# Hybrid streaming encoder: orders within a step, and the low parts of y's second chunk on GpSimd

## The chip, the cores and the metric

One core of a Trainium2 chip (trn2) runs one program: four layers of an encoder over 2048 positions. The metric is the device time of one execution in microseconds. TensorE (PE) multiplies, VectorE (DVE), ScalarE (ACT) and GpSimd (POOL) do elementwise work, SyncE (SP) issues the DMAs.

## The reference

x is 2048 x 1024, c a vector of 1024; everything is float32. What matters here:

```python
cond = silu(c)
for layer in range(4):          # RG-LRU, gated DeltaNet, causal pooling, windowed attention
    mod = cond @ ada_w[layer] + ada_b[layer]
    shift, scale, gate = split(mod, 3)
    h = rms_norm(x, norm_w[layer]) * (1.0 + scale) + shift
    y = mixer[layer](h)         # input projection, mixer, then y @ w_out (1024 x 1024)
    x = x + gate * y
return rms_norm(x, final_norm_w)
```

## The kernel before

The 2048 positions are done in two halves of 1024; a half lives in SBUF with features on the partitions (x, y and h are 8 tiles of 128 features x 1024 positions), and its positions are cut in two chunks of 512. A half runs through phases, one function each: `residual_phase` with layer -1 takes x in (transposes it and makes the first h), then for each layer a mixer phase (`rg_phase`, `dn_project_phase` and `dn_recur_phase`, `pool_phase`, `swa_phase`) and again `residual_phase`, which does the mixer's output projection, adds it to x, and makes the next layer's h (or, after the last layer, the output). In each phase every engine has its own program in a fixed order, and the engines wait for one another by semaphores; there is no planner. A phase's engines also wait at a fence until the others have left the phase before.

A float32 product of 128 x 128 weights and 128 x 512 activations is made of three matmuls (line 231): each operand is split in a high part (rounded to fp32r by ScalarE) and a low part (the difference), and hi*hi, hi*lo and lo*hi are summed. A projection's output tile ("a product") takes 8 x 3 matmuls. Weights come as tiles of 128 x 1024 through two raw buffers: SyncE loads (`load_to`), ScalarE rounds (`round_to`, line 204, which waits until the product that used the slot three tiles ago is done), GpSimd subtracts (`subtract_to`, line 213). The next raw load waits for that subtraction.

In an output projection (`residual_phase`) the steps j = 0 to 15 are (chunk c, feature tile d). The operand is y, whose high parts `round_y` makes on ScalarE (line 118) and whose low parts `lower_y` makes (line 127): those of the first chunk before the first step, the even tiles on VectorE and the odd on GpSimd; those of the second chunk in steps 0 to 7, one per step, alternating in the same way. Product 8 waits, tile by tile, for these. Products 0 and 1 are made together (line 250). Three PSUM banks are used in turn, so product j waits until product j - 3 has been added to x. In step j VectorE makes its low part if it has one, waits for product j, adds gate * product to x (line 781), adds the square of tile j - 1 to the running total (line 751; ScalarE makes the square, line 868), and in the second chunk makes a tile of the next h (lines 712 and 724). After product 8, TensorE sums the total of chunk 1 over the features (`sum_squares`, line 650, or line 646 after the last layer), for which it waits until square 7 is added.

After the last layer, ScalarE weights each x tile in place (line 870), TensorE turns it back with four transposes (`turn_x`, line 664), and the turn of tile j - 1 stands behind product j from j = 1 on. VectorE and ScalarE take the turned rows in turn, there is one buffer for a square, and the rows are scaled and stored.

The modulation cond @ ada_w is made in the first half by the class `Modulation`: `load` brings pieces of 128 rows of ada_w, `accumulate` has VectorE multiply each by its cond column and add it to a sum (lines 294 and 297), `reduce` has TensorE sum over the partitions (line 305), `finish` adds it to the vectors. It runs beside other work: shift and scale of layer 0 in the first ingest (16 pieces of 128 x 1024, in the space that h takes later), the rest in `rg_phase`, in layer 0's projection (`late`, 48 pieces of 128 x 512, four in each of steps 3 to 14) and in `pool_phase` (64 pieces of 128 x 512).

In `pool_phase` the products go by group g (4), part (u or gate), chunk c and tile t (2). VectorE does for each group the window sums and p of both chunks, each followed by a slot of six modulation pieces, then for each chunk the gate (line 2485), y, and another slot of six. TensorE reuses a gate's bank after line 2485, and makes the group product of p (line 2394) in between. SyncE loads three weight tiles ahead of the fence, the fourth behind it.

## Time and profile before

| | us |
|---|---|
| median of 3 timed runs | 3575.91 (3573.37 to 3576.22) |
| profiled execution | 3569.85 |
| its span | 3568.1 |
| TensorE busy, matmuls | 3316.8 (93%) |
| VectorE busy | 2307.7 (65%) |
| ScalarE busy | 1514.9 (42%) |
| GpSimd busy | 952.0 (27%) |
| mean granted TensorE clock | 0.967 of full |

The profile records one execution. Busy time is the sum of an engine's instructions; an instruction that stands because its engine cannot go on counts as busy too. "PEclk" is the TensorE clock that was granted, as a share of 2.4 GHz (0.5 is 1.2 GHz). In a timeline each instruction has its start and duration, and behind it in brackets the idle time of its engine before it and what released it. PEld is the weight load of a matmul.

### The profile page before, as it was taken

The page shows a single profiled execution, that of the slowest core. Times are in us where ns is not written, and L with a number is a line of the kernel's source. Part 1 is how long each engine was busy: PE and PEld are TensorE (multiplying, and loading weights), DVE is VectorE, ACT ScalarE, POOL GpSimd, SP SyncE. Part 2 cuts the span into 40 slices and gives each one's busy share as a digit, 9 for nine tenths or more (in the row PEclk, how much of TensorE's full clock was granted, in tenths as well). Part 3 has the DMA queues.
Part 4 walks back from the last instruction along what each step waited for, and adds up shares of the span by engine and source line. Part 5 has one row for each costly group of instructions (what it writes and reads, how often), then busy time and mean ns, then how long its engine had stood idle before and what let it go on. Part 6 is the DMA issues. An engine that isn't in the chain of part 4 may idle for free.

```text
span 3568.1 us, 49267 instructions
## 1 busy us (share of the span) xinstructions
PE 3316.8 (93%) x18911; PEld 2680.0 (75%) x18911; DVE 2307.7 (65%) x3812; ACT 1514.9 (42%) x2635; POOL 952.0 (27%) x495
## 2 busy tenths in 40 slices
PE   5998999799999999999889999988999999999998
PEld 3776688677887777888767777876778777788876
DVE  6887888763467765565457767896536564565553
ACT  4665365333344124323466655653334431342234
POOL 1003233211143124222510042432121421422243
PEclk7999899899999999999989999998999999999999
DMA  4434455444743523111231123554449211221112
GB/s 170 132 111 136 120 145 148 124 108 130 263 172 94 162 89 89 49 31 37 71 124 55 46 78 87 153 137 112 126 111 351 81 54 53 65 72 37 36 48 95
DMA packets 569015, 383.83 MB, mean 108 GB/s; under 512 B 67802, under 2 KB 522445, under 8 KB 568781
## 3 DMA queue, kind: packets, MB, share of 16 engines
q1 hardware_dynamic: 568781, 380.68, 35.7%
q8 instruction: 150, 2.46, 0.3%
q14 instruction: 84, 0.69, 0.1%
HBM read 299.01 MB, written 80.54 MB: 106 GB/s over the span
## 4 chain that ended last, share of the span: by engine, by line
PE 70%; DVE 16%; issue 4%; ACT 4%; DMA 4%; SPq 1%; POOL 1%; ACTq 0%; DVEq 0%; POOLq 0%
PE bank L231 52%; DVE dnp_conv L1866 3%; PE bank L250 2%; DVE dnp_diag_term L1944 2%; DVE h_lo L724 1%; PE bank L2394 1%; DVE dnp_diag_inv L1947 1%; PE bank L2603 1%; DMA dn_planes<-dnp_inv_t 1%; PE bank L2644 1%; PE bank L2630 1%; DVE res_h L712 1%; PE bank L1556 1%; DVE res_ada_sums L297 1%; POOL w_lo L213 1%
## 5 line engine op out<-in xcount | busy, mean ns | idle before, releaser
L231 PE MATMUL bank<-h_hi,w_hi 128*128 128x512 f32 x3488 | 1424.6, 408 | 39.3 <-DVE x_res L781 8.9
L231 PE MATMUL bank<-h_hi,w_lo 128*128 128x512 f32 x3488 | 1374.1, 394 | 0.0
L231 PE MATMUL bank<-h_lo,w_hi 128*128 128x512 f32 x3488 | 1373.4, 394 | 0.0
L213 POOL TENSOR_TENSOR w_lo<-w_raw,w_hi 128x1024 fp32r<-128x1024 f32 x262 | 651.4, 2487 | 1438.2 <-ACT w_hi L204 1437.6
L231 PEld LDWEIGHTS bank<-h_hi,w_hi 128*128 128x128 f32 x3488 | 664.5, 191 | 206.6 <-issue 27.9
L231 PEld LDWEIGHTS bank<-h_lo,w_hi 128*128 128x128 f32 x3488 | 665.5, 191 | 142.6 <-issue 12.8
L231 PEld LDWEIGHTS bank<-h_hi,w_lo 128*128 128x128 f32 x3488 | 663.3, 190 | 144.9
L204 ACT ACTIVATE w_hi<-w_raw 128x1024 fp32r<-128x1024 f32 x292 | 307.9, 1054 | 267.1 <-PE bank L231 128.8
L1866 DVE SCALAR_TENSOR_TENSOR dnp_conv<-dnp_raw,dn_conv_w,dnp_conv 128x512 f32<-128x512 f32 x288 | 265.6, 922 | 237.8 <-ACT dnp_conv L1688 230.4
L127 POOL TENSOR_TENSOR h_lo<-y,h_hi 128x512 fp32r<-128x512 f32 x72 | 102.2, 1432 | 501.9 <-ACT h_hi L118 501.3
L127 DVE TENSOR_TENSOR h_lo<-y,h_hi 128x512 fp32r<-128x512 f32 x56 | 100.5, 1814 | 153.8 <-ACT h_hi L118 153.7
L712 DVE SCALAR_TENSOR_TENSOR res_h<-x_res,mod_scale,res_rstd 128x512 f32<-128x512 f32 x128 | 148.2, 1164 | 58.2 <-ACT res_rstd L827 58.2
L781 DVE SCALAR_TENSOR_TENSOR x_res<-bank,mod_gate,x_res 128x512 f32<-128x512 f32 x128 | 94.9, 746 | 131.0 <-PE bank L231 130.7
L868 ACT ACTIVATE res_sq<-x_res 128x512 f32<-128x512 f32 x160 | 100.3, 627 | 142.6 <-DVE x_res L781 97.8
L734 ACT ACTIVATE h_hi<-res_h,mod_shift 128x512 fp32r<-128x512 f32 x128 | 91.9, 724 | 152.7 <-DVE res_h L712 151.7
L2587 POOL TENSOR_TENSOR swa_probs<-swa_probs,swa_tiny 128x1024 f32<-128x1024 f32 x32 | 60.8, 1900 | 335.3 <-DVE swa_tiny L2815 335.3
L1704 ACT ACTIVATE y<-dnp_conv 128x512 f32<-128x512 f32 x96 | 60.8, 633 | 174.0 <-DVE dnp_conv L1866 173.7
L1680 ACT ACTIVATE dnp_raw<-bank 128x512 f32<-128x512 f32 x96 | 56.8, 592 | 176.5 <-PE bank L231 172.9
L751 DVE TENSOR_TENSOR res_sq_total<-res_sq_total,res_sq 128x512 f32<-128x512 f32 x140 | 122.5, 875 | 10.0 <-ACT res_sq L868 9.4
L2788 DVE TENSOR_TENSOR swa_probs<-bank,swa_rel_bias 128x128 f32<-128x128 f32 x128 | 31.0, 285 | 148.7 <-PE bank L2618 148.6
L724 DVE SCALAR_TENSOR_TENSOR h_lo<-res_h,mod_shift,h_hi 128x512 fp32r<-128x512 f32 x128 | 121.6, 950 | 3.7 <-ACT h_hi L734 1.5
L2719 ACT ACTIVATE swa_probs<-swa_probs 128x1024 f32<-128x1024 f32 x32 | 34.0, 1062 | 169.4 <-DVE swa_probs L2805 169.4
(327 smaller groups left out, 4684.2 us busy)
## 6 DMA issues: line engine op xcount, KB each, us to landing
dnr_in<-dn_planes SPq DMA_DIRECT2D x112, 512.0 KB, 7.1
dn_planes<-y SPq DMA_DIRECT2D x192, 256.0 KB, 2.5
w_raw<-in_dn_w_in SPq DMA_DIRECT2D x64, 512.0 KB, 4.5
w_raw<-in_swa_w_in SPq DMA_DIRECT2D x36, 512.0 KB, 3.7
w_raw<-in_rg_w_in SPq DMA_DIRECT2D x32, 512.0 KB, 4.9
w_raw<-in_rg_w_out SPq DMA_DIRECT2D x32, 512.0 KB, 3.8
w_raw<-in_dn_w_out SPq DMA_DIRECT2D x32, 512.0 KB, 3.9
w_raw<-in_pool_w_in SPq DMA_DIRECT2D x32, 512.0 KB, 4.1
```

What stands on the lines that cost most here:

```text
L127: alu.tensor_tensor(self.h_lo[:, k, cols], self.y[:, k, cols], self.h_hi[:, k, cols].bitcast(F32), ALU.subtract).then_inc(self.y_split[k % ...
L204: self.nc.scalar.activation(self.hi[j % SLOTS][:, :, :], self.raw[j % 2][:, :, :], ACT.Copy).then_inc(self.rounded, 1)
L213: alu.tensor_tensor(self.lo[j % SLOTS][:, :, :], self.raw[j % 2][:, :, :], self.hi[j % SLOTS][:, :, :].bitcast(F32), ALU.subtract).then_in ...
L231: ins = self.nc.tensor.matmul(out, w[slot][:, k, :], x[:, k, cols], start=(k == 0 and n == 0), stop=(k == KT - 1 and n == 2))
L250: ins = self.nc.tensor.matmul(out, w[slot][:, k, :], x[:, k, cols], start=(k == 0 and m == 0), stop=(k == KT - 1 and m == 2))
L712: nc.vector.scalar_tensor_tensor(hf[m % NHF][:, :], x[:, k, cs[c]], core.modA[:, col:col + 1], rstd[:, :], op0=ALU.mult, op1=ALU.mult).the ...
L724: nc.vector.scalar_tensor_tensor(h_lo[:, k, cs[c]], hf[m % NHF][:, :], core.modB[:, col:col + 1], h_hi[:, k, cs[c]].bitcast(F32), op0=ALU. ...
L734: nc.scalar.activation(h_hi[:, k, cs[c]], hf[m % NHF][:, :], ACT.Identity, bias=core.modB[:, col:col + 1]).then_inc(s_hi, 1)
L751: nc.vector.tensor_tensor(total[c][:, :], total[c][:, :], sq[j % len(sq)][:, :], ALU.add).then_inc(s_add, 1)
L781: nc.vector.scalar_tensor_tensor(here, ring[j % len(ring)][:, :], core.modG[:, col:col + 1], here, op0=ALU.mult, op1=ALU.add).then_inc(s_x, 1)
L868: nc.scalar.activation(sq[j % len(sq)][:, :], x[:, d, cs[c]], ACT.Square).then_inc(s_sq, 1)
L1866: ins = V.scalar_tensor_tensor(conv[to][:, :], raw[r][:, k:k + CH], tap(par, k, n), conv[to][:, :], op0=ALU.mult, op1=ALU.add)
```

## The change

- In `residual_phase`, VectorE adds square j - 1 ahead of the addition of product j (but square 0 behind product 1), and no longer makes low parts of the second chunk: GpSimd makes all eight, one per step, behind the step's weight tile.
- After the last layer, the turns of tiles 0 and 1 both stand behind product 2; from there the turn of tile j - 1 stands behind product j, as before.
- In the first ingest, the scale of layer 0 is no longer summed on VectorE: its eight pieces of 128 x 1024 are multiplied by TensorE with the cond column as weights (two matmuls of 512 columns a piece, into banks 2 and 6, one piece in each of steps 4 to 11, behind the step's transposes), ScalarE copies the row of 1024, eight matmuls of one column turn it (bank 3), VectorE adds it. Scale and shift pieces are loaded in turn. The reduction of the shift and the turning stand ahead of the last sum of squares on TensorE.
- In `pool_phase`, SyncE loads four weight tiles ahead of the fence, and the modulation's pieces (now seven a slot) begin two slots later, after the first group's first y, with loads and reductions moved along.

```diff
+SCALE_BANKS, SCALE_FROM = (2, 6), 4
@@ residual_phase, sync
-                ada.load(sp, 0, ada.pieces)
+                for k in range(KT):
+                    sp.dma_start(scale_w[k], A["ada_w"][0, k * P:k * P + P, SCALE * D:SCALE * D + D]).then_inc(s_sw[k], 16)
+                    ada.load(sp, k, k + 1)
@@ residual_phase, tensor
+            def multiply_scale(k):
+                pe.wait_ge(s_sw[k], 16)
+                for i, b in enumerate(SCALE_BANKS):
+                    ins = nc.tensor.matmul(core.bank[b][0:1, :], core.cond[:, k:k + 1], scale_w[k][:, i * CH:i * CH + CH],
+                                           start=(k == 0), stop=(k == KT - 1))
+                if k == KT - 1:
+                    ins.then_inc(s_sm, 1)
+
+            def turn_scale():
+                pe.wait_ge(s_sr, len(SCALE_BANKS))
+                for m in range(KT):
+                    ins = nc.tensor.matmul(core.bank[3][:, KT + m:KT + m + 1], scale_row[0:1, m * P:m * P + P],
+                                           core.ones[0:1, 0:1], start=True, stop=True)
+                ins.then_inc(s_sc, 1)
...
+                    if ada and SCALE_FROM <= j < SCALE_FROM + KT:
+                        multiply_scale(j - SCALE_FROM)
...
-                if final and j > TURN_LAG - 1:
+                if final and j == 2:
+                    turn_x(0)
+                if final and j >= 2:
                     turn_x(j - TURN_LAG)
...
+            if ada:
+                for t in range(len(ada.blocks)):
+                    ada.reduce(pe, t)
+                turn_scale()
             if final or ada:
                 sum_squares(NCH - 1)
...
-            if ada:
-                for t in range(len(ada.blocks)):
-                    ada.reduce(pe, t)
@@ residual_phase, vector
-                if not ingest and c + 1 < NCH and d % 2 == 0:
-                    core.lower_y(dve, nc.vector, c + 1, [d])
+                if j > 1 or ingest and j:
+                    add_square(j - 1)
                 if not ingest:
                     dve.wait_ge(*projected(j))
                     here, col = x[:, d, cs[c]], layer * KT + d
                     nc.vector.scalar_tensor_tensor(here, ring[j % len(ring)][:, :], core.modG[:, col:col + 1],
                                                    here, op0=ALU.mult, op1=ALU.add).then_inc(s_x, 1)
-                if j:
-                    add_square(j - 1)
+                if not ingest and j == 1:
+                    add_square(0)
...
-                ada.accumulate(dve, KT, ada.pieces)
+                dve.wait_ge(s_sc, 1)
+                nc.vector.tensor_tensor(core.modS[:, here], core.bank[3][:, KT:2 * KT], core.modS[:, here], ALU.add)\
+                nc.vector.tensor_tensor(core.modA[:, here], core.modS[:, here], core.modA[:, here], ALU.mult).then_inc(s_sd, 1)
@@ residual_phase, scalar
+                act.wait_ge(s_sm, 1)
+                for i, b in enumerate(SCALE_BANKS):
+                    nc.scalar.activation(scale_row[0:1, i * CH:i * CH + CH], core.bank[b][0:1, :], ACT.Copy).then_inc(s_sr, 1)
@@ residual_phase, gpsimd
-                if not ingest and c + 1 < NCH and d % 2:
+                if not ingest and c + 1 < NCH:
                     core.lower_y(pool, nc.gpsimd, c + 1, [d])
@@ pool_phase
-            per = -(-ada.pieces // (4 * (NG - 1)))
+            per = -(-ada.pieces // (4 * (NG - 1) - GT))
...
-            w.load_to(sp, tile0 + 3)
+            w.load_to(sp, tile0 + 4)
...
-                    if ada:
-                        ada.load(sp, max(0, per * i - 3), per * i + 3)
+                    if ada and i >= GT:
+                        ada.load(sp, max(0, per * (i - GT - 1) + 3), per * (i - GT) + 3)
...
-                    if i == 2 * ((KT * m + KT - 1) // per) + 5:
+                    if i == 2 * ((KT * m + KT - 1) // per + GT) + 5:
...
-                    if ada and g < NG - 1:
-                        ada.accumulate(dve, per * (4 * g + c), per * (4 * g + c + 1))
+                    if ada and 0 < g < NG - 1:
+                        ada.accumulate(dve, per * (4 * g + c - GT), per * (4 * g + c - GT + 1))
...
-                        ada.accumulate(dve, per * (4 * g + 2 + c), per * (4 * g + 3 + c))
+                        ada.accumulate(dve, per * (4 * g + c), per * (4 * g + 1 + c))
```

## Rows read from the trace of the kernel before

**Rows 1.** the line of the low parts of y, by engine: duration ns min/median/max
```profile
L127 POOL TENSOR_TENSOR h_lo<-y,h_hi x72: 1268/1294/2344, 276.6 to 3507.9; 128x512 fp32r<-128x512 f32 x72
L127 DVE TENSOR_TENSOR h_lo<-y,h_hi x56: 679/1781/2524, 279.3 to 3499.0; 128x512 fp32r<-128x512 f32 x56
```

**Rows 2.** windows, two projections: start:end us, busy us of PE PEld DVE ACT POOL, PEclk, DMA
```profile
1340.00:1431.00 91.00, 88.96 (x388) 72.38 (x387) 53.90 (x52) 37.15 (x51) 42.64 (x20) 1.00 0.30 87
1712.00:1826.00 114.00, 101.93 (x496) 82.86 (x494) 42.24 (x54) 50.37 (x73) 48.11 (x24) 0.96 0.37 121
```

**Rows 3.** chain of waits, last layer, first half: start us, us, what
```profile
1729.81 7.54 PE bank L231 x24
...
1744.82 5.52 PE bank L231 x24
...
1779.93 6.40 PE bank L231 x24
```

**Rows 4.** timeline of TensorE there: start us, us, instruction [idle before it <- releaser]
```profile
1728.69 0.69 PE L664 MATMUL bank<-ident,x_res 128*128 128x128 f32 x2 [5.44 <-ACT x_res L870]
...
1757.16 0.66 PE L664 MATMUL bank<-ident,x_res 128*128 128x128 f32 x4 [0.91 <-ACT x_res L870]
...
1777.71 0.49 PE L646 MATMUL bank<-ones,res_sq_total 128*128 128x1 f32 x3 [1.44 <-DVE res_sq_total L751]
...
1824.68 0.55 PE L664 MATMUL bank<-ident,x_res 128*128 128x128 f32 x3 [2.34 <-ACT x_res L870]
```

**Rows 5.** timeline of the second half's layer 0: PE, DVE, POOL
```profile
2088.38 0.50 PE L231 MATMUL bank<-h_hi,w_hi 128*128 128x512 f32 x1 [4.04 <-DVE x_res L781]
...
2124.85 0.70 PE L650 MATMUL bank<-res_sq_total,ones 128*128 128x512 f32 x1 [1.44 <-DVE res_sq_total L751]
...
2097.62 2.72 DVE L751 TENSOR_TENSOR res_sq_total<-res_sq_total,res_sq 128x512 f32<-128x512 f32 x1
...
2084.77 2.34 POOL L213 TENSOR_TENSOR w_lo<-w_raw,w_hi 128x1024 fp32r<-128x1024 f32 x1 [8.23 <-ACT w_hi L204]
...
2099.75 1.74 POOL L127 TENSOR_TENSOR h_lo<-y,h_hi 128x512 fp32r<-128x512 f32 x1
...
2121.10 1.29 POOL L127 TENSOR_TENSOR h_lo<-y,h_hi 128x512 fp32r<-128x512 f32 x1
```

**Rows 6.** timeline of the first half's layer 0: PE, DVE, POOL
```profile
351.81 0.80 PE L231 MATMUL bank<-h_hi,w_hi 128*128 128x512 f32 x1 [6.57 <-POOL h_lo L127]
...
412.52 0.80 PE L305 MATMUL bank<-ones,res_ada_sums 128*128 128x1 f32 x3 [6.26 <-DVE res_ada_sums L297]
...
326.83 2.48 DVE L127 TENSOR_TENSOR h_lo<-y,h_hi 128x512 fp32r<-128x512 f32 x1 [0.32 <-ACT h_hi L118]
...
340.89 2.50 DVE L127 TENSOR_TENSOR h_lo<-y,h_hi 128x512 fp32r<-128x512 f32 x1 [0.30 <-ACT h_hi L118]
...
391.20 2.23 DVE L751 TENSOR_TENSOR res_sq_total<-res_sq_total,res_sq 128x512 f32<-128x512 f32 x1
...
390.40 2.49 POOL L213 TENSOR_TENSOR w_lo<-w_raw,w_hi 128x1024 fp32r<-128x1024 f32 x1 [4.61 <-ACT w_hi L204]
```

**Rows 7.** timeline of the first half's pooling layer: PE, DVE
```profile
1148.77 0.50 PE L231 MATMUL bank<-h_hi,w_hi 128*128 128x512 f32 x1 [3.63 <-POOL w_lo L213]
...
1162.58 0.79 PE L231 MATMUL bank<-h_hi,w_hi 128*128 128x512 f32 x1 [4.64 <-DVE pool_silu L2485]
...
1272.36 0.50 PE L231 MATMUL bank<-h_hi,w_hi 128*128 128x512 f32 x1 [0.73 <-DVE pool_silu L2485]
...
1169.64 0.75 DVE L297 SCALAR_TENSOR_TENSOR pool_ada_sums<-pool_ada,vectors,pool_ada_sums 128x512 f32<-128x512 f32 x1 [1.10 <-DMA pool_ada<-in_ada_w]
```

**Rows 8.** timeline of the start of the program: DVE, PE
```profile
49.66 9.62 DVE L297 SCALAR_TENSOR_TENSOR res_ada_sums<-before_h,vectors,res_ada_sums 128x1024 f32<-128x1024 f32 x7
...
63.55 0.75 DVE L712 SCALAR_TENSOR_TENSOR res_h<-x_res,mod_scale,res_rstd 128x512 f32<-128x512 f32 x1
...
45.67 2.08 PE L650 MATMUL bank<-res_sq_total,ones 128*128 128x512 f32 x2 [9.57 <-DVE res_sq_total L751]
```

More of the change, by code:

```diff
@@ L799, in _ @@
             if ada:
[L800 removed]
+                dve.wait_ge(s_sc, 1)
+                here = slice(0, KT)
+                nc.vector.tensor_tensor(core.modS[:, here], core.bank[3][:, KT:2 * KT], core.modS[:, here], ALU.add)\
+                    .then_inc(s_sd, 1)
+                dve.wait_ge(s_sd, 1)
+                nc.vector.tensor_tensor(core.modA[:, here], core.modS[:, here], core.modA[:, here], ALU.mult).then_inc(s_sd, 1)
+                dve.wait_ge(s_sd, 2)
                 ada.finish(dve)
```

11 lines of the change are left out of this document (9 added, 2 removed).

## The prediction

> **What bounds the kernel now.** I read the page first, then the waits of TensorE phase by phase, then the chain of waits and the timelines around each wait. The windows show the pattern: in the output projection of layer 2, TensorE is busy 88.96 of 91 us at full clock, so that only its few waits can be saved; in that of the last layer it is busy 101.93 of 114 at 0.96 [rows 2]. A product (24 matmuls) takes 5.5 us [rows 3]. So the question is which TensorE waits go, what they cost with the clock that they lower, and which new ones come. Every projection has products 0 to 7 (first chunk) and 8 to 15 (second); there are eight, four layers in two halves.
>
> **Last layer, order of TensorE and VectorE (twice).** TensorE now stands 5.44 us before the first turn of x, because product 0 has to be added, squared, weighted first [rows 4]. Product 2 needs none of that (its bank is free) and moves ahead of both turns; by its end ScalarE has done both squares. The wait goes: 5.44. The product behind it took 7.54 instead of 5.52 at the lowered clock [rows 3]: 2.02 more. Before each odd product's turn TensorE waits 0.91 [rows 4], three times per half: VectorE first makes a low part (held up by GpSimd's weight tile) and only then adds product j. With that low part on GpSimd the addition is immediate: 2.73. The sum of squares of chunk 1 waits 1.44 [rows 4], since VectorE adds product 8 before it adds square 7; in the new order square 7 was added while product 8 ran: 1.44, and 0.88 of clock behind it (6.40 against 5.52 [rows 3]). At the end, square 15 no longer waits for the addition of square 14, of the 2.34 [rows 4] some 0.65 (one such addition). What is late next is GpSimd: low part 7 follows weight tile 10 (product 7's end + 1.1 for ScalarE + 2.4 + 1.3 = 4.8), wanted at 5.3 here, as the turn gives half a us. Sum 13.2 per half, 26.4 in all. Bounds: 4.8 per half if the first turns only move their wait, 14.5 if nothing new is late.
>
> **The middle projections.** Layers 1 and 2 in both halves and layer 0 in the second: each has the same 1.44 [rows 5] at the sum of squares. But now the addition of square 7 comes early enough to meet GpSimd between its weight tile and low part 7. What happens then is in the trace: VectorE's addition stood 2.72 us while GpSimd worked, and the GpSimd low part behind it took 1.74 instead of 1.29 [rows 5], 0.45 later. Low part 7 already ends at 2122.39 [rows 5], when product 8 wants it. So 1.44 - 0.45 = 1.0 each, 5.0 together (bounds 3 and 7.2). Apart from that GpSimd's step is 2.4 + 1.3 = 3.7 of 5.5, and hides.
>
> **Layer 0, the fourth product.** It waits 4.04 for x [rows 5], as VectorE starts with a low part. Without it x is there 3.9 earlier, but weight tile 3 is only split at 2084.77 + 2.34 = 2087.11 [rows 5], so 1.2 is won, in the second half (0 to 3 with the clock).
>
> **Layer 0 of the first half.** Here VectorE also sums the modulation, four pieces per step, and is the bound: its low parts of steps 4 and 6 start 14.06 apart [rows 6], where two products and a reduction take 12. In such a pair it is occupied all the time, partly by standing: a weight tile on GpSimd from 390.40 to 392.89, and VectorE's addition from 391.20 to 393.43, that is, until just after it [rows 6]. So the two work in turn. The own time of a low part is 0.68 on VectorE and 1.29 on GpSimd [rows 1], so a pair of steps goes from (0.68 + 1.29) to 2.58 of shared time: +0.6, and up to +2.3 when the addition of x, which ran beside the weight tile, now comes behind the blocked square; 2.5 pairs, +1.5 to +5.6. In the second chunk the same lost overlap is 0 to 0.7 in six steps, 0 to +4.2. Against it: the stream starts 1.7 earlier, and the first sum of squares comes one addition (0.7) earlier. Net -0.9 to +7.4; I take +3.5, the middle, since VectorE never idles there. TensorE's 6.57 wait for low part 7 and the 6.26 at the end [rows 6] stay, as they are VectorE's lateness.
> The Trainium skill ("SBUF — State Buffer", section "SBUF: two separate sides") says that VectorE with two SBUF inputs and a GpSimd operation that reads SBUF exclude each other for the whole instruction. By that rule this layer gets slower; if they shared, it would get faster by some 3.5. It speaks against this part of the change, and the trace agrees with it.
>
> **Pooling layer, first half.** Three waits: 3.63 for weight tile 3, 4.64 and 0.73 for VectorE's gate [rows 7]. The tile is now loaded before the fence and is split when its slot comes free; gone. The second wait comes from twelve modulation pieces ahead of the first gates; they move behind, gone too, with some 2.0 of clock (as in the last layer). That is 11.0. But 64 pieces now lie in ten slots of 7 instead of eleven of 6. A piece costs 0.75, and every fourth waits for its DMA, 1.10 [rows 7]: about 1.1 a piece in the slot, three slots in series ahead of a gate, 3.3. The third group has no slack (0.73 was waited): 4.0. The second has some; I take 1.0 (0 to 3.3), and 0.9 for the clock. Net 11.0 - 5.9 = 5.1 (bounds 2 and 9). The second half has no pieces; counted at nothing.
>
> **Start of the program.** VectorE's scale pieces go: one of 0.74 and seven in 9.62, then reduction and last steps until 63.55, 4.3 after them [rows 8]. Instead TensorE multiplies, 16 matmuls of 512 columns. The trace has such a one as a pair in 2.08 at the low clock and about half at full [rows 8]. TensorE has turned x just before and runs at full clock, so I count 1.7 per step, less than two pieces of weight take to land (2.6); they pace it, to about 41. The first sum of squares stands in the queue behind the fifth of them, 7 us later than now; ScalarE and VectorE resume there and need 1.8 per step. The last shift sum ends near 51.9 (now 48.9), then 4.3 and a second set of eight small matmuls, 3.6: 59.8 against 63.55. The sum of squares of the second chunk, now behind these, has until well after the first low part. I take 3.5 saved; bounds: 6 saved, and 7 lost if all 16 ran at the low clock (33 us).
>
> **Sum.** -26.4 - 5.0 - 1.2 + 3.5 - 5.1 - 3.5 = -37.7. The profiled execution took 3569.85 (span 3568.1 and 1.75 around it): 3532.1. The median of the timed runs is 6.06 above it, so 3538.
>
> **Rivals.**
> The last layer only moves its wait: ScalarE does weight tile and rounding before each square, and the two turns behind product 2 wait for it. Against: its work for steps 0 and 1 adds to 5.5 from the end of product 1, just one product. Then 4.8 per half: 3538 + 16.8 = 3555. Chance 0.12.
> Start and pooling give nothing (low clock in the start, seven-piece slots): 3538 + 8.6 = 3547. Chance 0.13.
> GpSimd and VectorE hardly meet: layer 0 wins 3.5 instead of losing it, pooling wins 9: 3538 - 7.0 - 3.9 = 3527. For it: GpSimd is idle more than half of the time. Chance 0.14.
> Slower: low part 7 becomes the gate of product 8 in all eight projections as it is in the first half's layer 0, 6.57 each [rows 6], 52.6 together: 3591, with the clock more. It decides from the point where GpSimd's step (3.7 and what it stands for VectorE) passes a product's 5.5; it has 1.7 to spare. Chance 0.04.
> The change doesn't reach what binds (the waits named had another releaser behind them): within 7 of before. Chance 0.03.
>
> **Numbers.** The forecast, 3530 to 3545, has 0.54. Runs spread over 2.85 us, so 0.2% (7 us) is what can be told from no change. Faster 0.94, same 0.02, slower 0.04. Range 3525 to 3557: it leaves out the slow case and the far ends.
>
> **What would show it.** In the last layer the 5.44 and the 0.91 are gone and the third product takes 5.5; at each sum of squares no 1.44, but up to 0.6 in front of the last matmuls of product 8. Layer 0 of the first half is 0 to 7 longer. In pooling no wait at the first gates, one of some 4 in the third group. The first projection starts near 62. It is wrong if low part 7 is waited for by more than 1 us in the middle layers, or if product 2 of the last layer waits.

## The result and the profile after

The changed kernel takes 3516.0 us (median of 4, 3511.91 to 3519.31), the kernel before beside it 3574.89: ratio 0.9835, 95% interval 0.9818 to 0.9852. The profiled execution took 3519.31. It is faster, as forecast, but below the range: 3525 was its low end, 3538 the forecast. From profile to profile, where the prediction made its sum, the span goes from 3568.1 to 3517.5 us, -50.6; the medians differ by 58.9; forecast was -37.7.

The two windows of [rows 2], in the changed kernel, from each layer's first matmul (columns as there):

```profile
1329.90:1419.40 89.50, 88.46 (x386) 72.31 (x387) 57.19 (x48) 36.26 (x50) 50.11 (x24) 1.00 0.30 89
1698.60:1802.90 104.30, 101.50 (x518) 83.77 (x516) 58.52 (x54) 53.60 (x78) 58.48 (x28) 0.99 0.42 137
```

These windows and those of [rows 2] do not cover quite the same stretch. From the last layer's first matmul to its last sums, the first half in the kernel before and in the changed one:

```profile
1709.70:1825.17 115.47, 103.40 (x500) 83.95 (x497) 43.25 (x55) 51.25 (x74) 47.76 (x23) 0.96 0.36 117
```

```profile
1698.57:1798.87 100.30, 98.36 (x500) 81.09 (x497) 55.67 (x51) 50.27 (x74) 56.12 (x27) 1.00 0.41 129
```

The same 500 records of matmuls take 5.0 us less at the higher granted clock, and 10.1 us of idle time are gone. The chain of waits there, against [rows 3]:

```profile
1712.11 5.44 PE bank L231 x24
1717.56 0.87 PE bank L674 x8
1718.43 5.46 PE bank L231 x24
1723.89 0.44 PE bank L674 x4
...
1747.69 1.07 ACT w_hi L204
1748.76 0.07 issue
1748.83 2.40 POOL w_lo L213
1751.23 1.70 POOL h_lo L127
...
1753.94 0.79 PE bank L656 x8
1754.73 0.50 PE bank L674 x4
1755.22 5.48 PE bank L231 x24
```

The third product takes 5.44, both turns behind it come without a wait, and product 3 takes 5.46 where a product behind the wait took 7.54. Up to the layer's last turn the one place where other engines hold the chain is low part 7 behind weight tile 10 on GpSimd, as the prediction named it; TensorE's pause there is 0.14 us, too short to be told as a wait in the timeline. The last wait of the layer, 2.34 in [rows 4], is 1.68:

```profile
1798.38 0.66 PE L674 MATMUL bank<-ident,x_res 128*128 128x128 f32 x4 [1.68 <-ACT x_res L906]
```

The timeline of TensorE in both layers 0, against [rows 5] (second half, last two lines) and [rows 6] (first half):

```profile
304.18 0.47 PE L231 MATMUL bank<-h_hi,w_hi 128*128 128x512 f32 x1 [3.69 <-POOL w_lo L213]
...
346.26 0.80 PE L231 MATMUL bank<-h_hi,w_hi 128*128 128x512 f32 x1 [4.63 <-POOL h_lo L127]
349.12 1.22 PE L660 MATMUL bank<-res_sq_total,ones 128*128 128x512 f32 x1 [1.21 <-DVE res_sq_total L781]
...
405.35 1.87 PE L305 MATMUL bank<-ones,res_ada_sums 128*128 128x1 f32 x8 [4.62 <-DVE res_ada_sums L297]
...
2059.82 0.50 PE L231 MATMUL bank<-h_hi,w_hi 128*128 128x512 f32 x1 [2.91 <-POOL w_lo L213]
...
2094.28 0.50 PE L231 MATMUL bank<-h_hi,w_hi 128*128 128x512 f32 x1 [0.61 <-POOL h_lo L127]
```

In the second half the 4.04 has become 2.91 and changed its releaser from x to the weight tile, and the 1.44 at the sum of squares has become 0.61 at the low part, both as forecast; the other middle projections show the same 0.6. In the first half the 6.57 and the 6.26 are 4.63 and 4.62 here, but 6.35 and 9.05, and 5.51 and 4.61, in two more profiles of the changed kernel, so these two waits show no direction. The layer's length does: from its first matmul to its second sum of squares it is 127.8 to 130.2 us in four profiles with the new order and 131.2 to 134.3 in six with the old one. VectorE got earlier there, not later.

In the pooling layer the two waits at the start [rows 7] are gone, and two are there that were not, in all profiles of the changed kernel:

```profile
1201.09 0.50 PE L231 MATMUL bank<-h_hi,w_hi 128*128 128x512 f32 x1 [2.05 <-DVE pool_silu L2524]
...
1260.69 0.80 PE L231 MATMUL bank<-h_hi,w_hi 128*128 128x512 f32 x1 [5.27 <-DVE pool_silu L2524]
```

At the start of the program, against [rows 8], the scale products run at full clock (1.00 from 33 to 42 us). The two matmuls of a piece, which the profile records as four, take 1.88, and there is one piece per 2.4 with the transposes between:

```profile
36.08 0.66 PE L700 MATMUL bank<-ident,y 128*128 128x128 f32 x4
36.67 1.88 PE L681 MATMUL bank<-before_h,vectors 128*1 128x512 f32 x4
...
54.51 3.56 PE L689 MATMUL bank<-ones,res_scale_row 1*128 1x1 f32 x16
...
58.71 1.41 DVE L742 SCALAR_TENSOR_TENSOR res_h<-x_res,mod_scale,res_rstd 128x512 f32<-128x512 f32 x2
```

The norm's first operation starts at 58.71; it was 63.55.

Where the time went, by stretches of TensorE between marks that all kernels have (a projection's first matmul, its sums of squares; lengths read from the starts of these instructions). The third column is the difference of the two first profiles. Since stretches without any edit turned out to move by several us from one profile to the next, the last column takes the mean of two profiles of the kernel before and three of the changed one (the second and third are runs of the experiments below).

| stretch | forecast | first pair | means |
|---|---|---|---|
| start, to the first product | -3.5 | -4.8 | -4.4 |
| layer 0, first half | +3.5 | -2.9 | -2.8 |
| five middle projections (with the fourth product) | -6.2 | -7.8 | -8.4 |
| pooling, first half | -5.1 | -2.7 | -1.7 |
| pooling, second half | 0 | -1.0 | -1.0 |
| last layer, twice | -26.4 | -30.3 | -31.2 |
| stages without an edit, and the rest | 0 | -1.1 | -7.1 |
| sum | -37.7 | -50.6 | -56.6 |

Two and three profiles are few. Each stretch can also be read from every profile, of the experiments below too, in which all or none of its edits are present (5 to 8 profiles without, 4 to 11 with them). That gives -4.7 for the start, -3.3 for layer 0, -8.9 for the middle projections, -0.6 for pooling in the first half and -1.1 in the second, and -28.7 for the last layer.

### The profile page after: what moved, and what is told of

Same layout as the page of the kernel before. It is cut to its first block, busy times and chain, and to the rows that moved or that the text cites. A ratio compares the mean times of both kernels' runs of the same rounds, so it can differ in the third digit from the quotient of the medians.

```text
span 3517.5 us, 49319 instructions
## 1 busy us (share of the span) xinstructions
PE 3323.3 (94%) x18943; PEld 2681.9 (76%) x18943; DVE 2325.8 (66%) x3772; ACT 1507.3 (43%) x2637; POOL 1014.8 (29%) x527
## 4 chain that ended last, share of the span: by engine, by line
PE 75%; DVE 14%; DMA 3%; issue 3%; ACT 3%; POOL 1%; SPq 1%; DVEq 0%; ACTq 0%; POOLq 0%
PE bank L231 56%; DVE dnp_conv L1905 3%; PE bank L250 2%; DVE dnp_diag_term L1983 2%; PE bank L2433 1%; DVE dnp_diag_inv L1986 1%; PE bank L2642 1%; DVE h_lo L754 1%; PE bank L2683 1%; PE bank L2669 1%; PE bank L2203 1%; DVE res_ada_sums L297 1%; PE bank L1595 1%; POOL w_lo L213 1%; DVE res_h L742 1%
## 5 line engine op out<-in xcount | busy, mean ns | idle before, releaser
L204 ACT ACTIVATE w_hi<-w_raw 128x1024 fp32r<-128x1024 f32 x292 | 307.4, 1053 | 375.1 <-PE bank L231 222.7
L127 POOL TENSOR_TENSOR h_lo<-y,h_hi 128x512 fp32r<-128x512 f32 x104 | 164.3, 1588 | 502.9 <-ACT h_hi L118 502.3
L781 DVE TENSOR_TENSOR res_sq_total<-res_sq_total,res_sq 128x512 f32<-128x512 f32 x140 | 180.5, 1289 | 89.5 <-ACT res_sq L904 89.2
L754 DVE SCALAR_TENSOR_TENSOR h_lo<-res_h,mod_shift,h_hi 128x512 fp32r<-128x512 f32 x128 | 164.1, 1282 | 3.7 <-ACT h_hi L764 1.3
L742 DVE SCALAR_TENSOR_TENSOR res_h<-x_res,mod_scale,res_rstd 128x512 f32<-128x512 f32 x128 | 107.0, 842 | 51.7 <-ACT res_rstd L863 51.6
L2749 ACT ACTIVATE swa_q<-bank,swa_cur 128x512 f32<-128x512 f32 x32 | 22.0, 688 | 169.8 <-PE bank L231 169.7
```

Of the source, the lines that this page charges most:

```text
L127: alu.tensor_tensor(self.h_lo[:, k, cols], self.y[:, k, cols], self.h_hi[:, k, cols].bitcast(F32), ALU.subtract).then_inc(self.y_split[k % ...
L204: self.nc.scalar.activation(self.hi[j % SLOTS][:, :, :], self.raw[j % 2][:, :, :], ACT.Copy).then_inc(self.rounded, 1)
L742: nc.vector.scalar_tensor_tensor(hf[m % NHF][:, :], x[:, k, cs[c]], core.modA[:, col:col + 1], rstd[:, :], op0=ALU.mult, op1=ALU.mult).the ...
L754: nc.vector.scalar_tensor_tensor(h_lo[:, k, cs[c]], hf[m % NHF][:, :], core.modB[:, col:col + 1], h_hi[:, k, cs[c]].bitcast(F32), op0=ALU. ...
L781: nc.vector.tensor_tensor(total[c][:, :], total[c][:, :], sq[j % len(sq)][:, :], ALU.add).then_inc(s_add, 1)
```

## The experiments

Expectations call a theory by a letter that holds for that run alone. Runs of one group ran on one chip, beside the kernel before.

**First group: the edits of the step one by one.** The kernel before, with turns 0 and 1 behind product 2:

```
-                if final and j > TURN_LAG - 1:
+                if final and j == 2:
+                    turn_x(0)
+                if final and j >= 2:
                     turn_x(j - TURN_LAG)
```

> The kernel before with one edit: after the last layer the turns of tiles 0 and 1 both stand behind product 2. Theory A (the waits add up, each part on its own): per half 5.4 of wait, 2.0 of clock and 0.5 of a slow turn go, nothing else moves; 15 to 17 us faster than before in all, last layer 114.9 to about 107. Theory B (the recorded rival: the wait only moves unless the low parts move too): the two turns wait behind product 2, under 8 us faster in all.

The kernel before, with the square ahead of the low part and the addition:

```
+                if j > 1 or ingest and j:
+                    add_square(j - 1)
                 if not ingest and c + 1 < NCH and d % 2 == 0:
                     core.lower_y(dve, nc.vector, c + 1, [d])
...
-                if j:
-                    add_square(j - 1)
+                if not ingest and j == 1:
+                    add_square(0)
```

> The kernel before with one edit: VectorE adds square j-1 ahead of its low part and of the addition of product j. Theory A: the 1.44 at each of eight sums of squares goes, 0.45 of it comes back in front of the last matmuls of product 8 where GpSimd's low part 7 is pushed back, 0.65 goes at the end of each half: 8 to 13 us faster. Theory B (the shared time of VectorE and GpSimd decides): the early square meets GpSimd's tile and pushes it in every step, and what is won at the sum is lost there: within 4 us of before.

The kernel before, with all low parts of the second chunk on GpSimd (VectorE's two lines go, and GpSimd's condition loses `and d % 2`):

> The kernel before with one edit: all low parts of the second chunk of y on GpSimd. Theory A: the three waits of 0.91 per half in the last layer go (5.5), and 1.2 in layer 0 of each half; layer 0 of the first half is otherwise as long as before: 7 to 10 us faster. Theory B (as recorded in the prediction: shared time costs in layer 0 of the first half): that layer is 1.5 to 10 us longer than before, and the whole is within 4 us of before.

And the changed kernel with only this taken back, the low parts alternating as before:

> The changed kernel with one part undone: low parts of the second chunk alternate between VectorE and GpSimd as before, behind the early square. Theory A: the three waits of 0.91 per half and 1.2 in layer 0 of each half come back; 7 to 10 us slower than the changed kernel, 49 to 52 faster than before. Theory B (low parts on GpSimd cost in layer 0 of the first half): within 3 us of the changed kernel or faster, and layer 0 of the first half shorter than in the changed kernel's 123.7.

Measured, against 3570.01 us of the kernel before: turns 3557.97 (ratio 0.9963, 0.9950 to 0.9977), squares 3553.96 (0.9955, 0.9939 to 0.9971), low parts 3549.73 (0.9943, 0.9924 to 0.9962); turns and squares and the rest, without the low parts, 3534.99 (0.9902, 0.9882 to 0.9922). So 12, 16 and 20 us alone. None of the four is what either theory said of it: 15 to 17 or under 8 for the turns, 8 to 13 or under 4 for the squares, 7 to 10 or under 4 for the low parts, and for the last kernel 49 to 52 under the kernel before (it is 35.0 under) or no slower than the changed one by more than 3. The low parts have the largest median of the three, though the intervals (5 to 7 us to either side) overlap, whether they are added to the kernel before (20) or to the others (the changed kernel is 0.9858 on another chip, 15.7 less than 0.9902).

In the profiles, the last layer of both halves together takes 216.4 us with the turns alone, 218.9 with the squares, 211.2 with the low parts, 207.4 in the changed kernel without the low parts, and 200.6 in the changed kernel; in five profiles without any edit there it takes 226.6 to 232.8, mean 229.4. So the three edits are worth 13.0, 10.4 and 18.2 there alone, 41.6 in sum, but 28.7 together: they overlap.

The first turn of the last layer's first half, in these four in this order:

```profile
1739.60 1.11 PE L664 MATMUL bank<-ident,x_res 128*128 128x128 f32 x4 [1.94 <-ACT x_res L872]
```

```profile
1733.63 1.12 PE L664 MATMUL bank<-ident,x_res 128*128 128x128 f32 x4 [5.46 <-ACT x_res L872]
```

```profile
1733.52 0.66 PE L664 MATMUL bank<-ident,x_res 128*128 128x128 f32 x4 [2.18 <-ACT x_res L868]
```

```profile
1725.46 0.65 PE L674 MATMUL bank<-ident,x_res 128*128 128x128 f32 x4 [1.95 <-ACT x_res L908]
```

Only the changed kernel has nothing left of the 5.44. The low parts are needed for that beside the turns, as the last of the four shows (turns and low parts without the squares were not run): with the turns moved, 1.94 stay, because VectorE's first low part, 2.37 us long, stands ahead of its first addition of x. The chain of that kernel:

```profile
1732.64 2.37 DVE h_lo L127
1735.01 0.67 DVE x_res L783
...
1736.24 0.61 ACT x_res L872
```

So the prediction's "ScalarE has done both squares by the end of product 2" is true of the whole change and not of the turns alone. The three waits of 0.91, put down to the low parts, are gone in the kernel with the squares moved too, and in the kernel with the low parts moved: either does it. The last wait of 2.34 becomes 1.68 only where the squares are moved.

**Second group: start, pooling, and the cost of a low part.** The kernel before with the start's edit alone, and with the pooling edit alone (both as in the change's diff):

> The kernel before with the change at the start of the program alone (TensorE multiplies the scale part of the modulation). Theory A (this edit is worth what the trace of the changed kernel shows at that place, and nothing else in the program answers to it): the first product starts 4.8 us earlier (61.2 instead of 66.05) and everything behind keeps its length: -4.8 in the span, 3 to 6 in the medians. Theory B (an earlier or otherwise placed start also shifts the long DeltaNet stages, which take part of what the profile of the changed kernel had and the prediction had not): the first product is 4.8 earlier too, but the DeltaNet stages change by more than 2 us, and the span differs from -4.8 by as much.

> The kernel before with the change in the pooling phase alone. Theory A (the pooling phase is a cause of its own): from the sum of squares of the first half's layer 1 to layer 2's first matmul 220.1 becomes 217.4 (-2.7), and the same stretch of the second half 201.4 becomes 200.4 (-1.0, from the tile that is loaded ahead of the fence): -3.7 in all. Theory B (the -1.0 of the second half comes from the new order of the projection ahead of it): -2.7 alone. The prediction's term was -5.1 and 0.

The changed kernel with narrow low parts on GpSimd in the first half's layer 0:

```
-    def lower_y(self, eng, alu, c, ks):
+    def lower_y(self, eng, alu, c, ks, width=CH):
...
-                cols = slice(c * CH, c * CH + CH)
+                cols = slice(c * CH, c * CH + width)
...
-                    core.lower_y(pool, nc.gpsimd, c + 1, [d])
+                    core.lower_y(pool, nc.gpsimd, c + 1, [d], 8 if late else CH)
```

> The changed kernel, in which the low parts of y's second chunk in the first half's layer 0 (all on GpSimd) cover 8 columns instead of 512; the rest of these low parts is left out. Theory A (the prediction's: there VectorE and GpSimd work in turn, each low part on GpSimd takes its 1.29 us from VectorE's stream): VectorE's stream of modulation pieces and additions over the first chunk, 35.0 us in the changed kernel, shortens by 6 to 10, and the layer's 123.7 by as much or more. Theory B (a low part on GpSimd lies beside VectorE's reading of PSUM and its waits, and costs the stream next to nothing): the stream shortens by less than 2; the layer gets shorter only by TensorE's waits for low parts (4.6 for the seventh at the second chunk's start), so by 3 to 6 or less.

And the changed kernel again:

> The changed kernel once more. Theory A (the difference of the two profiles, 3568.1 to 3517.5, is the change's worth): 47 to 53 us under the median of the kernel before on the same chip. Theory B (the difference of the medians, 3574.89 to 3516.0, is): 56 to 62 under. The DeltaNet stages, where nothing is changed, should keep their lengths in this second profile if A's phase table is to be read to 1 us.

Measured, against 3569.95: start 3563.31 (0.9980, 0.9967 to 0.9992), its first product at 62.38, 3.7 earlier; pooling 3573.75 (1.0004, 0.9989 to 1.0019, no difference told); narrow low parts 3511.01 (0.9836, 0.9821 to 0.9851); the changed kernel 3518.67 (0.9858, 0.9841 to 0.9874), 51.3 under, theory A's value here; but the same pair is 58.9 and, in the fourth group, 56.2 apart. The medians of the five edits alone make -12.0 - 16.0 - 20.3 - 6.6 + 3.8 = -51.1, near the whole change. That doesn't show that the edits are independent: each median is uncertain by some 5 us, and in the last layer three of them overlap by 13.

The start's kernel showed what the profile of one execution hides: behind the start nothing is edited, and its first DeltaNet stage took 610.1 us where the first profile of the kernel before has 604.2, at 0.96 of granted clock instead of 0.97; it is theory B's case, except that the other experiments show the same with other edits, so it isn't the start that does it. The pooling kernel's second-half stage is 200.4 against 201.4, so that -1.0 is the earlier weight tile's. Its first half took 219.8 against 220.1 where -2.7 was expected.

With narrow low parts VectorE's stream (from the first modulation piece to the third block's first, two pairs of steps with four low parts) took 24.5 us instead of 29.2, and the layer up to the second sum of squares 122.87 instead of 128.35. So GpSimd's low part does take from VectorE, 4.7 / 4 = 1.2 us each here, 1.0 from the changed kernel's mean of 28.3 (three profiles): theory A's sharing is real, if smaller than its 6 to 10 (which it gave for the whole first chunk: up to the first sum of squares the layer takes 60.75 us instead of 65.21). That left open why moving them there costs nothing.

**Third group: what a low part costs on VectorE.** The kernel before with VectorE's four narrowed in that layer, `core.lower_y(dve, nc.vector, c + 1, [d], 8 if late else CH)`; the changed kernel with alternating low parts in that layer alone; and two attempts at a faster one:

> The kernel before, in which VectorE's low parts of y's second chunk in the first half's layer 0 (steps 0, 2, 4, 6) cover 8 columns instead of 512; the rest of these low parts is left out. Measured is the stretch of VectorE's stream from the first modulation piece to the third block's first piece (two pairs of steps, two of these low parts), 30.1 to 34.8 us, mean 31.9, in the profiles in which the low parts alternate. Theory A (the prediction's: a low part costs VectorE its own 0.68): the stretch gets 1.4 shorter. Theory B (a low part on VectorE comes just as GpSimd starts a weight tile, and stands behind it; it costs VectorE's stream 0.68 and most of the 1.8 that it stands, more than the 1.03 by which each low part on GpSimd lengthened the stream in the kernel with narrow low parts): 3.5 to 5 shorter, 27 to 28.5.

> The changed kernel with the low parts alternating between VectorE and GpSimd again in the first half's layer 0 alone. Theory A (the prediction's +1.5 to +5.6 for the low parts on GpSimd there): 2 to 4 us faster than the changed kernel. Theory B (they cost less on GpSimd): 1 to 3 us slower. Everything else as in the changed kernel, to 1 us.

```
+                if not ingest and c + 1 < NCH and j > 1:
+                    core.lower_y(pool, nc.gpsimd, c + 1, [d])
                 if not ingest:
                     w.subtract_to(pool, min(tile0 + j + 4, tile0 + len(steps) + 2))
-                if not ingest and c + 1 < NCH:
+                if not ingest and j < 2:
                     core.lower_y(pool, nc.gpsimd, c + 1, [d])
```

(ScalarE's `round_y` and `round_to` likewise.)

> The changed kernel; from the third step on, ScalarE rounds the part of y before the weight tile, and GpSimd makes the low part before the weight tile's. It aims at TensorE's waits for low part 7 (4.6 in the first half's layer 0, 0.6 in the four other projections that are not the last, 1.7 twice in the last layer). If the low part is late only because it stands behind the weight tile: these waits go, 3 to 9 us in all, since the weight tiles have two products of slack. If VectorE's stream is what binds the first half's layer 0, its wait turns up elsewhere and 3 to 5 remain. Rival: the low part now comes alone and again between VectorE's operations, which makes VectorE stand twice per step instead of once: the first half's layer 0 gets 2 to 6 longer.

```
-            per = -(-ada.pieces // (4 * (NG - 1) - GT))
+            per = -(-ada.pieces // (4 * (NG - 1) - GT + 1))
...
-                    if ada and 0 < g < NG - 1:
+                    if ada and g:
...
-                if ada and g == NG - 1:
-                    ada.finish(dve)
...
+            if ada:
+                ada.finish(dve)
             core.leave(dve, "dve")
```

> As the kernel with the low parts ahead of the weight tiles, and the pooling phase with six pieces per slot in eleven slots instead of seven in ten; the modulation's last step moves to the phase's end. If the slots of seven are what TensorE waited for in the changed kernel (2.06 and 5.27 us in the third and fourth group), 2 to 7 us less than the kernel with that edit alone; if the gates are late for the pooling windows themselves, no change within 1.5.

Measured, against 3573.43: narrow on VectorE 3567.92 (0.9984, 0.9971 to 0.9996); alternating in that layer 3520.0 (0.9842, 0.9826 to 0.9859); low parts ahead of the weight tiles 3516.82 (0.9836, 0.9817 to 0.9856); with six pieces 3511.25 (0.9818, 0.9802 to 0.9834). The first is told by its timeline, VectorE and GpSimd:

```profile
325.88 2.39 POOL L213 TENSOR_TENSOR w_lo<-w_raw,w_hi 128x1024 fp32r<-128x1024 f32 x1 [1.31 <-ACT w_hi L204]
...
326.36 1.93 DVE L127 TENSOR_TENSOR h_lo<-y,h_hi 128x8 fp32r<-128x8 f32 x1 [0.38 <-ACT h_hi L118]
...
339.95 1.94 DVE L127 TENSOR_TENSOR h_lo<-y,h_hi 128x8 fp32r<-128x8 f32 x1 [0.38 <-ACT h_hi L118]
```

Eight columns take 1.93 us, and 512 took 2.48 [rows 6]: the width is worth 0.55, and the rest is standing until the weight tile ends, at 325.88 + 2.39 = 328.27, where the narrow one ends at 328.29. The stream took 29.4: 0.7 under the first profile's 30.1, 2.7 under the mean of 32.1. That is not theory B's 27 to 28.5, and with such a spread no proof of theory A's 1.4; the two rows decide instead. The standing belongs to the weight tile and hits whatever VectorE has next.

With the low parts ahead of the weight tiles, the 0.61 is gone in each middle projection (0.9 us shorter each). In the first half's layer 0 the wait for the low part is gone too, and is back in full one instruction later; TensorE there:

```profile
348.43 2.07 PE L660 MATMUL bank<-res_sq_total,ones 128*128 128x512 f32 x2 [7.41 <-DVE res_sq_total L781]
```

7.41 stands where 4.63 and 1.21 stood: VectorE binds this layer, and low part 7 was its shadow. In the profiles the five middle projections take 467.1 us where the changed kernel's mean is 470.4, and the last layer 199.8 for 200.6. That is 4.1 together, inside the 3 to 5 that the expectation left for the case that VectorE binds this layer. The median is 3.2 under the alternating kernel's on this chip, which is within both spreads. The rival's longer layer did not come (128.6 us), though VectorE does stand more: its stretch takes 30.2, and 29.1 in the next kernel, where the changed kernel has 27.6 to 29.2.

With six pieces the pooling layer's waits are 1.78 and 2.33:

```profile
1199.84 0.54 PE L231 MATMUL bank<-h_hi,w_hi 128*128 128x512 f32 x1 [1.78 <-DVE pool_silu L2526]
...
1257.16 0.50 PE L231 MATMUL bank<-h_hi,w_hi 128*128 128x512 f32 x1 [2.33 <-DVE pool_silu L2526]
```

(The expectation calls these groups third and fourth; they are the second and the third.) That is 5.6 us in the medians, inside the expected 2 to 7, and the layer's stretch goes from 219.2 to 215.5 us. 3511.25 (3509.97 to 3515.35) is the lowest of all kernels that leave nothing out. It is 5 to 7 us under the three medians of the changed kernel, which were taken on other chips.

**Fourth group: the two terms that were still unsized.** The changed kernel with the old pooling phase; the changed kernel again; the changed kernel with the whole old step order in the first half's layer 0 alone; and a second profile of the kernel before:

> The changed kernel with the pooling phase as it was before. Theory A (the prediction's: -5.1 for the first half, nothing for the second): 5 us slower than the changed kernel on the same chip. Theory B (what single profiles say: -2.7 and -1.0): 3 to 4 slower. Theory C (slots of seven pieces give back all that the first gates win): 1 slower, from the second half alone.

> The changed kernel, as the partner of the others on this chip: 3510 to 3522.

```
-                if j > 1 or ingest and j:
+                if (j > 1 or ingest and j) and not late:
                     add_square(j - 1)
+                if late and c + 1 < NCH and d % 2 == 0:
+                    core.lower_y(dve, nc.vector, c + 1, [d])
...
-                if not ingest and j == 1:
-                    add_square(0)
+                if late and j or not ingest and j == 1:
+                    add_square(j - 1)
...
-                if not ingest and c + 1 < NCH:
+                if not ingest and c + 1 < NCH and (d % 2 or not late):
                     core.lower_y(pool, nc.gpsimd, c + 1, [d])
```

> The changed kernel with the whole order of the kernel before in the first half's layer 0 alone (low parts alternating, square behind low part and addition). Theory A (the prediction's +3.5 for the new order there): 3.5 us faster than the changed kernel. Theory B (the new order shortens that layer, as the profiles say): 1 to 4 us slower.

> The kernel before once more, for its profile. If the stages without an edit keep their lengths to 1 us, differences of single profiles can be read as effects of the edits; if the DeltaNet and pooling stages move by 2 us or more, as they do between the experiments, only waits that are named and repeat can be.

Measured, against 3573.85: old pooling 3522.63 (0.9850, 0.9836 to 0.9863), the changed kernel 3517.62 (0.9839, 0.9826 to 0.9853), old order in layer 0 3521.84 (0.9851, 0.9836 to 0.9865). That is 5.0 and 4.2 above the changed kernel, but the runs themselves overlap (3517.07 to 3523.18 and 3517.74 to 3525.38 against 3515.29 to 3521.96), so the medians don't tell either from nothing. For layer 0 the profiles have the sign: the kernel with the old order has 131.3 us for the layer, among the other five of that order and above all four of the new one. For pooling in the first half they say little: its stretch takes 220.1 us in the mean of eight profiles with the old phase (217.6 to 222.7) and 219.5 in the mean of nine with the new one (217.3 to 220.5). The second half's 201.4 for 200.4 is there each time, to 0.4. That is nearest to the third theory, by which the slots of seven give back what the first gates win. Layer 0 up to the second sum of squares, in the kernel with the old order, and in the changed kernel beside it (windows, columns as in [rows 2]):

```profile
282.71:414.06 131.35, 106.52 (x447) 85.85 (x447) 105.84 (x119) 49.93 (x67) 47.69 (x22) 0.88 0.54 161
```

```profile
283.46:411.27 127.81, 108.77 (x446) 87.18 (x447) 104.77 (x115) 49.70 (x67) 55.69 (x26) 0.89 0.56 165
```

The second profile of the kernel before has a span of 3579.9. Its long DeltaNet stage of the first half, and that of the first profile:

```profile
419.77:1029.93 610.16, 560.35 (x3573) 465.12 (x3571) 401.95 (x859) 268.21 (x628) 149.66 (x88) 0.95 0.52 155
```

```profile
420.00:1024.19 604.19, 550.82 (x3573) 457.45 (x3571) 408.17 (x859) 268.35 (x628) 150.29 (x88) 0.97 0.53 156
```

Same kernel, same instructions, 6 us and two hundredths of granted clock apart.

## Why the prediction was right or wrong

**Last layer: right in place, 13.2 against 15.2 per half in the first pair** (14.3 in the means over seven and five profiles). The waits behind 5.44, 0.91, 1.44 and 2.34 did what was said, to 0.1 us. Mis-sized was the clock behind a wait: only the product was counted (2.02, 0.88), not the turns and sums that also run slow there. They are 0.66 against 0.44 (three turns), 1.12 against 0.44 (the first), 1.26 against 0.79 (the sums) and 0.96 against 0.50: 0.66 + 0.68 + 0.47 + 0.46 = 2.3. It fits that idle time fell by 10.1, for 10.3 forecast, and busy time by 5.0, for 2.9. The cause of the 0.91 was half right (above). The rival in which the wait only moves is true in part of the turns alone, where 1.94 of it stay behind product 2; in the changed kernel none does. Its 4.8 per half was also summed too low: without the 5.44 and the 2.02 the terms make 5.7.

**Middle projections: right in kind, 6.2 against 7.8.** Low part 7 is the next to be late in each, 0.61 against the 0.45 taken from the blocked operation. Layer 2 shows 1.3 for the 1.0 in both halves, in all profiles of the changed kernel. By the starts of its matmuls that is 1.62 won at the sum, 0.43 lost at the low part and 0.1 won as the sum itself no longer runs slow: a wait moved the next matmul by some 0.2 more than its idle time, and that was not counted. The fourth product's 4.04 became 2.91, 1.13 for 1.2.

**Layer 0 of the first half: the step that failed.** The prediction said that VectorE and GpSimd work in turn there, so that each pair of steps gets 0.6 to 2.3 longer, and the second chunk 0 to 4.2. The premise held: the narrow kernel shows 1.0 to 1.2 per low part on GpSimd for the 1.29 assumed. The Trainium skill ("SBUF — State Buffer", section "SBUF: two separate sides") has a VectorE operation with two SBUF inputs and a GpSimd operation that reads SBUF exclude each other for the whole instruction. The rows agree (below), but the sum for this layer was wrong all the same. What failed is the balance. A pair of steps took 32.1 / 2 = 16.1 us in the old order (mean of six profiles, stretches of 30.1 to 34.8) and 28.2 / 2 = 14.1 in the new one (four profiles, 27.6 to 29.2): 2.0 shorter, where 0.6 to 2.3 longer was forecast, and the layer is 3.3 us shorter (131.2 to 134.3 us in six profiles, 127.8 to 130.2 in four). Over the two pairs VectorE's own work falls by 1.4 (two low parts), its idle time from 2.8 to 1.3 and its standing behind GpSimd from 11.8 to 10.7 (time beyond each form's own duration, summed over the records), though GpSimd does two operations more. In the prediction's model the standing had to grow by about what GpSimd got. It doesn't. A likely reason is that GpSimd's low part comes right behind its weight tile: in the two kernels with the low part ahead of the tile the stretch was 30.2 and 29.1. The two, in the changed kernel, with VectorE's operations beside them:

```profile
320.52 0.74 DVE L811 SCALAR_TENSOR_TENSOR x_res<-bank,mod_gate,x_res 128x512 f32<-128x512 f32 x1
321.18 8.25 DVE L297 SCALAR_TENSOR_TENSOR res_ada_sums<-res_ada,vectors,res_ada_sums 128x512 f32<-128x512 f32 x4
...
320.89 2.40 POOL L213 TENSOR_TENSOR w_lo<-w_raw,w_hi 128x1024 fp32r<-128x1024 f32 x1 [2.30 <-ACT w_hi L204]
323.25 1.74 POOL L127 TENSOR_TENSOR h_lo<-y,h_hi 128x512 fp32r<-128x512 f32 x1
326.51 2.37 POOL L213 TENSOR_TENSOR w_lo<-w_raw,w_hi 128x1024 fp32r<-128x1024 f32 x1 [1.52 <-ACT w_hi L204]
328.84 1.71 POOL L127 TENSOR_TENSOR h_lo<-y,h_hi 128x512 fp32r<-128x512 f32 x1
```

An addition of x, which reads PSUM, keeps its 0.74 beside a weight tile, and the square's addition behind it does not. In the kernel before:

```profile
333.57 2.47 POOL L213 TENSOR_TENSOR w_lo<-w_raw,w_hi 128x1024 fp32r<-128x1024 f32 x1 [4.81 <-ACT w_hi L204]
333.72 0.74 DVE L781 SCALAR_TENSOR_TENSOR x_res<-bank,mod_gate,x_res 128x512 f32<-128x512 f32 x1
334.38 2.21 DVE L751 TENSOR_TENSOR res_sq_total<-res_sq_total,res_sq 128x512 f32<-128x512 f32 x1
```

In the old order a low part that reads SBUF twice came first behind ScalarE's rounding, at the tile's start (326.83 + 2.48 in [rows 6]), and held the addition of x and all behind it for 2.4 us; in the new one such an operation no longer stands there by construction. That this is where the 2 us per pair come from fits the records, but was not isolated: alternating the low parts back in this layer alone cost nothing that can be told (3520.0; its layer takes 128.6 us, and its stretch, 30.1, lies between the two means). On the kernel before, the low parts alone give a stretch of 30.3 and a layer of 130.8, the squares alone 32.7 and 133.8, one profile each. Why the standing does not grow, and how the gain is shared between squares and low parts, stay open.

The point where I chose was the error: ends of -0.9 and +7.4 were written as the bounds, the middle taken (it is 3.25, not 3.5) "since VectorE never idles there", and the lower bound assumed that nothing but a low part's own 0.68 leaves VectorE. The rival "GpSimd and VectorE hardly meet", -3.5 for this layer, gave the right size by a wrong reason: VectorE still stands 10.7 us in two pairs.

**Pooling: first half overrated, second half missed.** 5.1 were forecast for the first half. The first pair has 2.7 and the means 1.7, but all profiles together have 0.6, and the medians of the fourth group can't settle it. The two waits at the start went as said; what was too small is the price of the slots of seven: the wait in the third group was forecast at some 4 and is 5.27, that in the second at 1.0 and is 2.05, and the two make 7.0 to 8.3 in six profiles with the new phase. In the kernels with the old one the wait of 4.64 is itself between 1.1 and 4.6, so there is not always as much to win. The second half's 1.0, from the tile loaded ahead of the fence, was counted at nothing though the same wait of 3.63 in the first half was on the page.

**Start: right in kind,** 3.5 against 4.7: the first product starts at 60.96 to 62.74 in eleven profiles with the edit and at 66.05 to 66.97 in seven without it. The steps came as written, most of them a little sooner (the norm at 59.8 in the forecast, at 58.71 in the profile).

**What no step names.** The rest, 7.1 in the means, lies mostly in the DeltaNet stages: 607.2 to 606.8 in the first half and 610.4 to 605.7 in the second. Over all profiles, eight of kernels built on the one before and ten on the changed one, they are 2.7 and 1.4 shorter. No instruction is changed there, and the spread within one kernel is 6; whether a projection that ends sooner or otherwise sets the clock of what follows, or it is chance, stays open. And the bound of "2.85 us" for the spread of runs, from three, was far too small: 60 runs of the kernel before lie between 3563.59 and 3583.19, median 3573.0, while 13 of the changed kernel lie between 3511.91 and 3521.96, median 3517.6. That is a difference of 55.4, and the forecast of -37.7 missed it by 18. In the table's means the miss is 6.3 by layer 0 of the first half, 4.8 by the last layer, 2.2 by the middle, 0.9 by the start, 7.1 by what no step names, less 2.4 in pooling, together 18.9 of the means' 56.6. Over all profiles the last layer's part is only 2.3, so that more of it belongs to no step.

## What to carry to other kernels

Price a wait with everything that runs slow behind it, the small matmuls too: here that was 2 us more in each half's last layer than the product alone. An operation on a busy engine costs what it holds up, not its own duration: eight columns cost 1.93 us on VectorE where 512 cost 2.48, since it stood for GpSimd's tile; so ask what comes to the head of the queue when GpSimd starts. And before small terms are read from two profiles, take a second profile of the same kernel: here stages without an edit moved by 6 us.

## What the runs showed of the hardware

A VectorE operation with two inputs in SBUF that started beside a GpSimd weight tile or low part, more than 0.75 us before its end, always stood until that one was done. In the kernel before all 16 such additions of squares, and in the changed kernel all 59, took 1.35 to 2.89 instead of 0.68 and ended 0.54 to 0.55 us after the GpSimd operation. An operation of 8 columns stood as well, and ended 0.02 after it (328.29 against 328.27). The additions of x, with one input in PSUM, kept their 0.74 to 0.75 in all 11 and 18 such cases.

GpSimd's own low part, right behind a weight tile and with VectorE waiting, takes 1.74 instead of 1.29. That fits one VectorE operation let in between: the piece that waits in the rows above ends at 323.84, 0.55 after the tile, inside the low part's 323.25 to 324.99.

The granted clock of one kernel's stage can differ by 0.02 between executions, with the same instructions (0.97 and 0.95 in the DeltaNet stage above).
